# The output's scale and shift in an RWKV-7 recurrence: scale into ScalarE's copy, shift onto the bonus, on one Trainium2 core

## The chip, the cores and the metric

The kernel runs on one core of a Trainium2 chip. The metric is the device time of one execution in microseconds. Of the kernel before, three executions were timed: 2039.26, 2049.12 and 2057.95 us, median 2049.12.

The names in rows and code: PE is TensorE, DVE is VectorE, ACT is ScalarE, POOL is GpSimd, SP is SyncE, which issues the loads.

## The reference, cut to what matters

The program is a chain of an RWKV-7 mixer, a short convolution and a second block. The change concerns the mixer alone. It has 512 positions and 2048 inner channels, in 32 heads of 64.

```python
y = wkv7_scan(rh, heads(decay), kh, vh, kk, kk * ah)
y = head_group_norm(y, lnx_w, lnx_b)       # (y - mean) * rsqrt(var + GN_EPS) * w + b, per head of 64
bonus = (jnp.sum(rh * kh * r_k, axis=-1, keepdims=True) * vh)
y = (y + bonus.reshape(bsz, t, D_INNER)) * jax.nn.silu(g)
out = y @ w_out
```

So each output channel gets a scale w and a shift b after its normalisation, then the bonus is added, then the gate multiplies. The scale and the shift are constants per channel.

## The kernel before, in words

Channels lie on partitions, 128 at a time, which is two heads; positions lie on the free axis. `rwkv_phase` walks over 16 such pairs of heads (`IC` = 16), and a step of its loop works on three pairs at once: it solves the recurrence of pair c by chunks of 64 positions, it prepares the keys, rates, decays and values of pair c+1, and it finishes the outputs of pair c-1. Each engine has its own written-out program of the step, and semaphores tie them together. No scheduler reorders anything: an engine does its operations in the order of the code, and one that waits holds all behind it.

What a step does on each engine, as far as the change and the prediction speak of it:

- TensorE: the scores of pair c (L995, 64 matmuls with `bet`, then 64 with `kd`), five levels of the chunk inverse (L1021 and L1033), in between parts of the dense products for the keys and the values of pair c+1 (L949 to L953). The products for the keys go into the bank `GK`, which `bonus` of pair c was read from, so they wait for `bonus`. In the last step the output projection fills these places instead (L1083 to L1089), and it waits for `y_hi` and `y_lo`, the two halves of the gated outputs.
- VectorE: it begins with `invT` (L1382), read from the scores, then masks and adds of the five levels (L1368, L1373) with copies of the state (L1342) between them. Then come the preparations of pair c+1: `kk` (L1286), `tha` (L1303), `phi` and `rh` (L1439, L1441), `rt` (L1291), `kap` (L1309), `bet` (L1316), `kd` (L1278), and last `bonus` (L1322) and a first state copy. `bonus` has two buffers, used in turn. The one that step c writes for pair c+1 is the one that pair c-1 used, and it is free when the addition of pair c-1 has read it (semaphore `plus`).
- ScalarE: copies from PSUM and the activation functions. `outputs` (L838, L839) copies the outputs of pair c-1 to `yc` and their squares to `yv`; the mean has already gone from the values. Later `output_log` and `output_root` make the inverse deviation in `yv` (semaphore `yrs`). The copies `swapT` (L832) belong to the levels of the inverse.
- GpSimd: a mask (L711), the splits of three tiles in a high and a low half (`halved`, L641 and L644), small products (L666, L672, L677), a split of weights (L689), and at the end of the step the tail of pair c-1, `finished`: `yc` times `yv` (L695), scale and shift (L698), plus the bonus (L702), times the gate (L705). Between two of its operations it waits for the semaphore of the one before.

Pairs 14 and 15 have their tail on VectorE (`finished` there, L1326, L1329, L1332). In the last step GpSimd splits the gated outputs instead (`y_lo`, L660).

`mixpar` holds eight numbers per channel; `chan(c, 6)` is the column of the scales of pair c and `chan(c, 7)` that of its shifts, both already halved for the gate. SyncE's loads are not touched by the change; they wait for `rt`, `bon` and the splits.

Of the kernel before, what the change touches and what calls it, by code (L numbers as in the profile page):

```python
# [6 lines left out]
ALU = mybir.AluOpType  # L7
ACT = mybir.ActivationFunctionType
# [100 lines left out]
def apart(eng):  # L109

    eng.nop(nofuse=True)
# [406 lines left out]
def rwkv_phase(K):  # L518
    nc, ins, bank, psum, C, V = (K[n] for n in ("nc", "ins", "bank", "psum", "C", "V"))
    eps, gate, lerp, hidden, mixpar, sbt = (K[n] for n in ("eps", "gate", "lerp", "hidden", "mixpar", "sbt"))  # L520
    out_raw, out_hi, out_lo = K["ring"]
    y, D = K["y"], K["dense"]
    with ExitStack() as ctx:
        S = Sems(nc, ctx, "mix")
# [4 lines left out]
        def placed(name):  # L529
            at = -(-nc.sbuf_base // 32) * 32  # L530
            return sbt(ctx, name, [P, T]), at
# [5 lines left out]
        rt, bonus = sbt(ctx, "rt", [P, 2, T]), sbt(ctx, "bonus", [P, 2, T])  # L537
# [28 lines left out]
        yc = sbt(ctx, "yc", [P, T])  # L566
        yv, yv_at = placed("yv")
# [6 lines left out]
        chan = lambda n, i: mixpar[:, n, i:i + 1]  # L574
# [15 lines left out]
        parity = lambda ap: ap.rearrange("p (b j t) -> p b j t", j=2, t=HD)  # L590
# [17 lines left out]
        def more(c):  # L608

            return not (isinstance(c, int) and c >= IC - 2)  # L610
# [24 lines left out]
        def _(pool):  # L635
# [11 lines left out]
            def key_halves(n):  # L647
                need(pool, S("kd"), n)
                need(pool, S("bet"), n)
                halved("nsq", n)  # L650
# [35 lines left out]
            def key_weights(n):  # L686
# [2 lines left out]
                pool.tensor_scalar(wts["k"][0][:, :], raw["k"][:, :], 1.0, 0.0, ALU.mult, ALU.add)\  # L689
                    .then_inc(S("whi_k"), 1)  # L690

            def finished(c, p):
                pool.wait_ge(S("yrs"), c + 1)
                apart(pool)
                pool.tensor_tensor(yc[:, :], yc[:, :], yv[:, :], ALU.mult).then_inc(S("yn"), 1)  # L695
                pool.wait_ge(S("yn"), c + 1)
                apart(pool)
                pool.tensor_scalar(yc[:, :], yc[:, :], chan(c, 6), chan(c, 7), ALU.mult, ALU.add).then_inc(S("affine"), 1)  # L698
                pool.wait_ge(S("affine"), c + 1)
                pool.wait_ge(S("bonus"), c + 1)  # L700
                apart(pool)
                pool.tensor_tensor(yc[:, :], yc[:, :], bonus[:, p, :], ALU.add).then_inc(S("plus"), 1)  # L702
                pool.wait_ge(S("plus"), c + 1)
                apart(pool)
                pool.tensor_tensor(gate[:, c, :], gate[:, c, :], yc[:, :], ALU.mult).then_inc(S("gated"), 1)  # L705

            def reads_masked(c):
                pool.wait_ge(S("la"), 2 * c + 2)
                pool.wait_ge(S("inv0"), 2 * c + 2)
                apart(pool)  # L710
                pool.tensor_tensor(LA[:, :, :, 1, :], LA[:, :, :, 1, :], over2(C["score_mask"][:, HD:2 * HD]), ALU.mult)\  # L711
                    .then_inc(S("la_reads"), 1)

            def step(c, p=None):
                q = c % 2 if p is None else p
                last = c == IC - 1
                reads_masked(c)
                if not last:
                    key_halves(c + 1)
                    prepare(c + 1, 1 - q)  # L720
                if last:
                    pool.wait_ge(S("inv0"), 2 * IC)
                    out_halves(range(10))
                if c > 0:
                    halved("ysq", c - 1)
                if not last:
                    rate(c + 1)
                if more(c):
                    key_weights(c + 2)
                if not last:  # L730
                    read_halves(c + 1)
                    chunk_ends(c + 1, 1 - q)
                    if c > 0:
                        finished(c - 1, 1 - q)
# [12 lines left out]
        def _(act):  # L747
# [86 lines left out]
            def outputs(c):  # L834
                act.wait_ge(S("y_mm"), c + 1)
                need(act, S("gated"), c)
                y_banks = psum[:, 2:4, 0:half].rearrange("p j (b t) -> p b j t", t=HD)
                act.activation(parity(yc[:, :]), y_banks, ACT.Copy).then_inc(S("y"), 1)  # L838
                act.activation(parity(yv[:, :]), y_banks, ACT.Square).then_inc(S("ysq"), 1)  # L839

            def out_split(g):
# [9 lines left out]
            def step(c, p=None):  # L851
# [25 lines left out]
                if not first:  # L877
                    outputs(c - 1)
# [377 lines left out]
        def _(dve):  # L1256
# [67 lines left out]
            def finished(c, p):  # L1324
                dve.wait_ge(S("yrs"), c + 1)
                dve.tensor_tensor(yc[:, :], yc[:, :], yv[:, :], ALU.mult).then_inc(S("yn"), 1)  # L1326
                dve.wait_ge(S("yn"), c + 1)
                dve.wait_ge(S("bonus"), c + 1)
                dve.scalar_tensor_tensor(out=yv[:, :], in0=yc[:, :], scalar=chan(c, 6), in1=bonus[:, p, :],  # L1329
                                         op0=ALU.mult, op1=ALU.add).then_inc(S("plus"), 1)  # L1330
                dve.wait_ge(S("plus"), c + 1)
                dve.scalar_tensor_tensor(out=gate[:, c, :], in0=yv[:, :], scalar=chan(c, 7), in1=gate[:, c, :],  # L1332
                                         op0=ALU.add, op1=ALU.mult).then_inc(S("gated"), 1)

            def masked(dst, src, sem):
                dve.tensor_tensor(dst.rearrange("p b k t -> p b (k t)"), pairs(src), over(C["score_mask"], TB),
# [1163 lines left out]
```

## Time and profile before

| | us |
|---|---|
| median of three timed executions | 2049.12 |
| their lowest and highest | 2039.26, 2057.95 |
| the profiled execution | 2050.97 |
| its span, first to last instruction | 2049.2 |
| mean granted TensorE clock | 0.971 |
| recurrence, first `bonus` to last `bonus` start | 270.1 to 807.1 |

The profile shows one execution by engine, with start and duration of each instruction, the idle time before it and what released it. All stretches and starts below are microseconds from the start of the span. A number in square brackets at the end of a row of a timeline is idle time of that engine just before the instruction.

### The profile page before, as it was taken

To read this page: it belongs to the slowest core of one execution; us is meant where nothing else is said; L and a number is where in the kernel's file an instruction comes from. 1 tells how busy PE (TensorE), PEld (TensorE's weight loads), DVE (VectorE), ACT (ScalarE), POOL (GpSimd) and SP (SyncE) were. 2 spreads that over 40 slices of the span, in tenths; PEclk is the share of its full clock that TensorE was granted. 3 is DMA by queue.
4 is the path that set the end of the run, shared out by engine and by line. 5 is a ranking of instruction groups with operands and counts; after the bars stand their busy time and mean duration, and the time that the engine had idled before them with its cause. 6 is when DMAs were issued, how large, how long until landed. Compare 5 with 4: busy or idle time off the path is not lost.

```text
span 2049.2 us, 43917 instructions
## 1 busy us (share of the span) xinstructions
PE 1890.1 (92%) x18912; PEld 1480.9 (72%) x18912; DVE 1234.7 (60%) x1755; ACT 899.7 (44%) x1400; POOL 313.7 (15%) x298
## 2 busy tenths in 40 slices
PE   4999789999999999799999999999887699999997
PEld 3677567767766677588888888887665478888885
DVE  6562177777777777344555555445557577777522
ACT  5342256656565567333222222334445354444321
POOL 3000034535455355300000000000000000000000
PEclk9999899999999999999999999999999799999998
DMA  3224311111111011142322223221110032323331
GB/s 123 78 83 142 109 48 39 44 35 41 46 41 45 30 41 43 49 155 93 101 95 95 100 93 102 89 98 62 52 42 21 21 114 93 103 92 99 91 94 67
DMA packets 51455, 154.15 MB, mean 75 GB/s; under 512 B 8513, under 2 KB 11073, under 8 KB 51265
## 3 DMA queue, kind: packets, MB, share of 16 engines
q1 hardware_dynamic: 51264, 151.35, 22.8%
q8 instruction: 151, 2.47, 0.5%
q14 instruction: 40, 0.32, 0.0%
HBM read 145.04 MB, written 6.29 MB: 74 GB/s over the span
## 4 chain that ended last, share of the span: by engine, by line
PE 51%; DVE 4%; ACT 1%; issue 0%; DVEq 0%; ACTq 0%
PE bank L1670 15%; PE bank L1669 15%; PE bank L1671 15%; PE bank L1757 1%; PE bank L1758 1%; PE bank L1759 1%; DVE room L2381 0%; PE bank L1794 0%; DVE room L2348 0%; PE bank L1777 0%; PE bank L1838 0%; PE bank L1829 0%; PE bank L1740 0%; PE bank L1805 0%; PE bank L1802 0%
## 5 line engine op out<-in xcount | busy, mean ns | idle before, releaser
L1876 ACT ACTIVATE w_hi<-raw 128x1024 fp32r<-128x1024 f32 (+2 forms) x195 | 197.8, 1015 | 504.7 <-PE bank L1671 458.9
L1669 PE MATMUL bank<-h_hi,w_hi 128*128 128x512 f32 x896 | 349.8, 390 | 0.0
L1671 PE MATMUL bank<-h_hi,w_lo 128*128 128x512 f32 x896 | 348.6, 389 | 0.0
L1670 PE MATMUL bank<-h_lo,w_hi 128*128 128x512 f32 x896 | 348.6, 389 | 0.0
L151 DVE TENSOR_TENSOR w_lo<-raw,w_hi 128x1024 fp32r<-128x1024 f32 (+2 forms) x202 | 236.8, 1173 | 154.7 <-ACT w_hi L1876 154.3
L1670 PEld LDWEIGHTS bank<-h_lo,w_hi 128*128 128x128 f32 x896 | 168.2, 188 | 35.6 <-issue 0.7
L1669 PEld LDWEIGHTS bank<-h_hi,w_hi 128*128 128x128 f32 x896 | 168.2, 188 | 35.3 <-issue 0.7
L1671 PEld LDWEIGHTS bank<-h_hi,w_lo 128*128 128x128 f32 x896 | 168.2, 188 | 35.0
L144 PE MATMUL bank<-xg_hi,g_hi 128*128 128x512 f32 x256 | 103.4, 404 | 21.4 <-DVE g_lo L151 11.8
L1651 POOL TENSOR_SCALAR room<-room 128x512 f32<-128x512 f32 x4 | 3.5, 880 | 703.0 <-ACT room L1945 703.0
L832 ACT ACTIVATE swapT<-invT 64x256 f32<-64x256 f32 x192 | 79.8, 416 | 56.8 <-DVE invT L1373 52.9
L145 PE MATMUL bank<-xg_lo,g_hi 128*128 128x512 f32 x256 | 101.9, 398 | 0.0
L146 PE MATMUL bank<-xg_hi,g_lo 128*128 128x512 f32 x256 | 101.6, 397 | 0.0
L151 DVE TENSOR_TENSOR g_lo<-g_raw,g_hi 128x1024 fp32r<-128x1024 f32 x32 | 40.7, 1276 | 88.1 <-ACT g_hi L302 88.0
L1669 PE MATMUL bank<-y_hi,w_hi 128*128 128x512 f32 x224 | 89.2, 398 | 1.3 <-PEq L134 1.3
L1670 PE MATMUL bank<-y_lo,w_hi 128*128 128x512 f32 x224 | 89.8, 401 | 0.0
L1671 PE MATMUL bank<-y_hi,w_lo 128*128 128x512 f32 x224 | 89.1, 398 | 0.0
L1368 DVE TENSOR_TENSOR low<-bank,con 128x512 f32<-128x512 f32 x80 | 55.3, 691 | 53.9 <-PE bank L1021 53.9
L1373 DVE TENSOR_TENSOR invT<-invT,bank 128x512 f32<-128x512 f32 x80 | 55.0, 687 | 52.4 <-PE bank L1033 52.4
L144 PEld LDWEIGHTS bank<-xg_hi,g_hi 128*128 128x128 f32 x256 | 49.6, 194 | 38.6 <-DVE g_lo L151 13.5
L1021 PEld LDWEIGHTS bank<-inv,LA 64*64 64x64 f32 x2560 | 46.0, 135 | 42.5 <-issue 42.5
L302 ACT ACTIVATE g_hi<-g_raw 128x1024 fp32r<-128x1024 f32 x32 | 33.8, 1058 | 90.7 <-PE bank L146 90.5
(390 smaller groups left out, 4363.9 us busy)
## 6 DMA issues: line engine op xcount, KB each, us to landing
raw<-in_w_conv SPq DMA_DIRECT2D x64, 512.0 KB, 3.2
raw<-in_w_up SPq DMA_DIRECT2D x44, 512.0 KB, 3.2
raw<-in_w_out SPq DMA_DIRECT2D x32, 512.0 KB, 3.8
raw<-in_w_in SPq DMA_DIRECT2D x20, 512.0 KB, 3.2
g_raw<-in_w_g SPq DMA_DIRECT2D x16, 512.0 KB, 3.2
g_raw<-in_w_r SPq DMA_DIRECT2D x16, 512.0 KB, 3.7
w_k<-in_w_k SPq DMA_DIRECT2D x16, 512.0 KB, 4.2
w_v<-in_w_v SPq DMA_DIRECT2D x16, 512.0 KB, 3.5
```

What stands on the lines that cost most here:

```text
L144: pe.matmul(out, w_hi[:, w], x_hi[:, k, :], start=(first and n == 0), stop=False)
L145: pe.matmul(out, w_hi[:, w], x_lo[:, k, :], start=False, stop=False)
L146: m = pe.matmul(out, w_lo[:, w], x_hi[:, k, :], start=False, stop=(last and n == len(ks) - 1))
L151: return dve.tensor_tensor(lo, full, hi.bitcast(F32), ALU.subtract)
L832: act.activation(swapT[rows[1 - j], :, :], invT[rows[j], 1, :, :], ACT.Copy).then_inc(S("swap"), 1)
L1021: m = pe.matmul(X[h][rows[j ^ h], cols(b)], LA[rows[j], h, b, 0, :], inv[rows[j], h, b, :], start=True, stop=True)
L1368: dve.tensor_tensor(low[:, :, :, :], heads(0), over2(C["level_mask"][:, lv * HD:(lv + 1) * HD]), ALU.mult).then_inc(S("low"), 1)
L1373: up = dve.tensor_tensor(invT[:, :, :, :], invT[:, :, :, :], heads(half), ALU.add)
L1669: pe.matmul(to, whi, hi, start=begin, stop=False)
L1670: pe.matmul(to, whi, lo, start=False, stop=False)
L1671: last = pe.matmul(to, wlo, hi, start=False, stop=end)
L1876: act.activation(w_hi[:, g % RING, 0:width], raw[:, g % RAW, 0:width], ACT.Copy).then_inc(S("whi"), 1)
```

## The change

The scale is put into ScalarE's copy of the outputs (`yc`), which had none before; `yv`, the squares, is still made from the outputs without it. The shift is added to the finished bonus of the pair by a new operation on GpSimd, `raised`, in the next step behind the mask. The pass that did both in GpSimd's tail goes. The two tails on VectorE lose their scale and shift as well, and become a plain sum and a plain product. The semaphore `affine` goes, `raised` comes in.

```diff
--- before.py
+++ after.py
@@ -689,15 +689,18 @@
                 pool.tensor_scalar(wts["k"][0][:, :], raw["k"][:, :], 1.0, 0.0, ALU.mult, ALU.add)\
                     .then_inc(S("whi_k"), 1)
 
+            def raised(c, p):
+                pool.wait_ge(S("bonus"), c + 1)
+                apart(pool)
+                pool.tensor_scalar(bonus[:, p, :], bonus[:, p, :], chan(c, 7), 0.0, ALU.add, ALU.add)\
+                    .then_inc(S("raised"), 1)
+
             def finished(c, p):
                 pool.wait_ge(S("yrs"), c + 1)
                 apart(pool)
                 pool.tensor_tensor(yc[:, :], yc[:, :], yv[:, :], ALU.mult).then_inc(S("yn"), 1)
                 pool.wait_ge(S("yn"), c + 1)
-                apart(pool)
-                pool.tensor_scalar(yc[:, :], yc[:, :], chan(c, 6), chan(c, 7), ALU.mult, ALU.add).then_inc(S("affine"), 1)
-                pool.wait_ge(S("affine"), c + 1)
-                pool.wait_ge(S("bonus"), c + 1)
+                pool.wait_ge(S("raised"), c + 1)
                 apart(pool)
                 pool.tensor_tensor(yc[:, :], yc[:, :], bonus[:, p, :], ALU.add).then_inc(S("plus"), 1)
                 pool.wait_ge(S("plus"), c + 1)
@@ -715,6 +718,7 @@
                 q = c % 2 if p is None else p
                 last = c == IC - 1
                 reads_masked(c)
+                raised(c, q)
                 if not last:
                     key_halves(c + 1)
                     prepare(c + 1, 1 - q)
@@ -835,7 +839,7 @@
                 act.wait_ge(S("y_mm"), c + 1)
                 need(act, S("gated"), c)
                 y_banks = psum[:, 2:4, 0:half].rearrange("p j (b t) -> p b j t", t=HD)
-                act.activation(parity(yc[:, :]), y_banks, ACT.Copy).then_inc(S("y"), 1)
+                act.activation(parity(yc[:, :]), y_banks, ACT.Copy, scale=chan(c, 6)).then_inc(S("y"), 1)
                 act.activation(parity(yv[:, :]), y_banks, ACT.Square).then_inc(S("ysq"), 1)
 
             def out_split(g):
@@ -1325,12 +1329,10 @@
                 dve.wait_ge(S("yrs"), c + 1)
                 dve.tensor_tensor(yc[:, :], yc[:, :], yv[:, :], ALU.mult).then_inc(S("yn"), 1)
                 dve.wait_ge(S("yn"), c + 1)
-                dve.wait_ge(S("bonus"), c + 1)
-                dve.scalar_tensor_tensor(out=yv[:, :], in0=yc[:, :], scalar=chan(c, 6), in1=bonus[:, p, :],
-                                         op0=ALU.mult, op1=ALU.add).then_inc(S("plus"), 1)
+                dve.wait_ge(S("raised"), c + 1)
+                dve.tensor_tensor(yc[:, :], yc[:, :], bonus[:, p, :], ALU.add).then_inc(S("plus"), 1)
                 dve.wait_ge(S("plus"), c + 1)
-                dve.scalar_tensor_tensor(out=gate[:, c, :], in0=yv[:, :], scalar=chan(c, 7), in1=gate[:, c, :],
-                                         op0=ALU.add, op1=ALU.mult).then_inc(S("gated"), 1)
+                dve.tensor_tensor(gate[:, c, :], gate[:, c, :], yc[:, :], ALU.mult).then_inc(S("gated"), 1)
 
             def masked(dst, src, sem):
                 dve.tensor_tensor(dst.rearrange("p b k t -> p b (k t)"), pairs(src), over(C["score_mask"], TB),
```

On GpSimd the order of a middle step is, before (`yc` is the output, `LA` the masked scores of the next step, `nn_hi` the split of the key norms behind it):

```order
L683 TENSOR_SCALAR ends<-decays 128x8 [waits mix_exp,mix_st]
L695 TENSOR_TENSOR yc<-yc,yv 128x512 [waits mix_yrs]
L698 TENSOR_SCALAR yc<-yc,mixpar 128x512 [waits mix_yn]
L702 TENSOR_TENSOR yc<-yc,bonus 128x512 [waits mix_affine,mix_bonus]
L705 TENSOR_TENSOR gate<-gate,yc 128x512 [waits mix_plus]
L711 TENSOR_TENSOR LA<-LA,con 128x8x64 [waits mix_la,mix_inv0]
L641 TENSOR_SCALAR nn_hi<-nn 128x512 [waits mix_nsq,mix_kd,mix_bet]
```

and now:

```order
L683 TENSOR_SCALAR ends<-decays 128x8 [waits mix_exp,mix_st]
L701 TENSOR_TENSOR yc<-yc,yv 128x512 [waits mix_yrs]
L705 TENSOR_TENSOR yc<-yc,bonus 128x512 [waits mix_yn,mix_raised]
L708 TENSOR_TENSOR gate<-gate,yc 128x512 [waits mix_plus]
L714 TENSOR_TENSOR LA<-LA,con 128x8x64 [waits mix_la,mix_inv0]
L695 TENSOR_SCALAR bonus<-bonus,mixpar 128x512 [waits mix_bonus]
L641 TENSOR_SCALAR nn_hi<-nn 128x512 [waits mix_nsq,mix_kd,mix_bet]
```

The sum with `bonus` follows the product at once, and the pass over `mixpar` stands two places later, on another tile.

On VectorE the tail of pair 14 in the last step was:

```order
L151 TENSOR_TENSOR w_lo<-raw,w_hi 128x1024 [waits dense_whi]
L1326 TENSOR_TENSOR yc<-yc,yv 128x512 [waits mix_yrs]
L1329 SCALAR_TENSOR_TENSOR yv<-yc,mixpar,bonus 128x512 [waits mix_bonus,mix_yn]
L1332 SCALAR_TENSOR_TENSOR gate<-yv,mixpar,gate 128x512 [waits mix_plus]
L1439 TENSOR_TENSOR phi<-bank,con 128x3x64 [waits mix_phi_mm]
```

and is now:

```order
L151 TENSOR_TENSOR w_lo<-raw,w_hi 128x1024 [waits dense_whi]
L1330 TENSOR_TENSOR yc<-yc,yv 128x512 [waits mix_yrs]
L1333 TENSOR_TENSOR yc<-yc,bonus 128x512 [waits mix_raised,mix_yn]
L1335 TENSOR_TENSOR gate<-gate,yc 128x512 [waits mix_plus]
L1441 TENSOR_TENSOR phi<-bank,con 128x3x64 [waits mix_phi_mm]
```

The places are the same, the operations have two operands instead of three.

## Rows read from the trace of the kernel before

**Rows 1.** The page: busy time, share of the span and instructions of each engine.

```profile
PE 1890.1 (92%) x18912; PEld 1480.9 (72%) x18912; DVE 1234.7 (60%) x1755; ACT 899.7 (44%) x1400; POOL 313.7 (15%) x298
```

**Rows 2.** Waits, 230 to 880 us: engine line <- released by: us, times, longest.

```profile
DVE bonus L1322 <- POOL yc L702: 15.2, 12, 1.3
...
PE bank L995 <- issue: 7.5, 6, 2.0
...
PE bank L1089 <- POOL y_lo L660: 3.5, 4, 1.6
```

**Rows 3.** Timeline of GpSimd, step 8: start us, us, instruction [idle before <-releaser].

```profile
581.84 1.29 POOL L695 TENSOR_TENSOR yc<-yc,yv 128x512 f32<-128x512 f32 x1
583.31 2.05 POOL L698 TENSOR_SCALAR yc<-yc,mixpar 128x512 f32<-128x512 f32 x1 [0.18 <-POOL yc L695]
...
602.98 0.62 POOL L641 TENSOR_SCALAR nn_hi<-nn 128x512 fp32r<-128x512 f32 x1 [11.78 <-ACT nn L777]
```

**Rows 4.** Timeline of VectorE over the same tail.

```profile
582.86 0.81 DVE L1291 TENSOR_TENSOR rt<-rraw,decays 128x512 f32<-128x512 f32 x1
583.60 0.68 DVE L1309 TENSOR_TENSOR kap<-kk,decays 128x512 f32<-128x512 f32 x1
584.20 0.68 DVE L1316 TENSOR_TENSOR bet<-tha,cum 128x512 f32<-128x512 f32 x1
584.80 1.09 DVE L1278 TENSOR_TENSOR kd<-kp,cum 128x512 f32<-128x512 f32 x1
587.16 0.69 DVE L1322 TENSOR_TENSOR bonus<-bank,vT 128x512 f32<-128x512 f32 x1 [1.26 <-POOL yc L702]
...
587.96 0.68 DVE L1382 TENSOR_TENSOR invT<-bank,con 128x512 f32<-128x512 f32 x1
```

**Rows 5.** Timeline of TensorE, the scores of the next pair.

```profile
585.42 0.27 PE L995 MATMUL bank<-kap,bet 64*64 64x64 f32 x2
...
586.27 0.33 PE L995 MATMUL bank<-rt,bet 64*64 64x64 f32 x8
```

**Rows 6.** Timeline of all engines, the tail of step 11.

```profile
693.97 1.07 DVE L1291 TENSOR_TENSOR rt<-rraw,decays 128x512 f32<-128x512 f32 x1
...
694.67 1.51 POOL L702 TENSOR_TENSOR yc<-yc,bonus 128x512 f32<-128x512 f32 x1 [0.17 <-POOL yc L698]
...
694.96 1.78 DVE L1309 TENSOR_TENSOR kap<-kk,decays 128x512 f32<-128x512 f32 x1
...
696.33 1.54 POOL L705 TENSOR_TENSOR gate<-gate,yc 128x512 f32<-128x512 f32 x1
...
696.66 1.75 DVE L1316 TENSOR_TENSOR bet<-tha,cum 128x512 f32<-128x512 f32 x1
...
698.57 0.40 PE L995 MATMUL bank<-kap,bet 64*64 64x64 f32 x8 [1.71 <-DVE bet L1316]
...
698.95 0.68 DVE L1322 TENSOR_TENSOR bonus<-bank,vT 128x512 f32<-128x512 f32 x1
```

**Rows 7.** Groups of ScalarE: xcount | busy us, mean ns | idle before.

```profile
L838 ACT ACTIVATE yc<-bank 128x512 f32<-128x512 f32 x13 | 7.9, 605 | 9.5 <-PE bank L1065 9.5
...
L771 ACT ACTIVATE kk<-bank,mixpar 128x512 f32<-128x512 f32 x11 | 7.6, 687 | 18.3 <-PE bank L953 18.3
```

**Rows 8.** Timeline of ScalarE in step 8.

```profile
575.79 0.86 ACT L832 ACTIVATE swapT<-invT 64x256 f32<-64x256 f32 x2 [0.39 <-DVE invT L1373]
```

**Rows 9.** Group of VectorE, its own tails.

```profile
L1329 DVE SCALAR_TENSOR_TENSOR yv<-yc,mixpar,bonus 128x512 f32<-128x512 f32 x2 | 1.5, 751 | 0.1
```

**Rows 10.** Stretches: us, busy (x) of PE, PEld, DVE, ACT, POOL, PEclk, DMA, GB/s.

```profile
697.50:700.00 2.50, 1.44 (x57) 1.47 (x61) 2.31 (x4) 0.00 (x0) 0.37 (x1) 0.75 0.63 205
700.00:702.50 2.50, 2.07 (x78) 1.95 (x71) 1.93 (x3) 1.25 (x3) 0.02 (x1) 0.57 0.02 7
```

**Rows 11.** Timeline of TensorE, the longest pause inside its scores.

```profile
446.26 0.21 PE L995 MATMUL bank<-kap,kd 64*64 64x64 f32 x1 [2.02 <-issue]
```

**Rows 12.** The stretch around and behind that pause, columns as in rows 10.

```profile
445.00:481.00 36.00, 33.71 (x859) 25.84 (x858) 26.88 (x44) 21.91 (x41) 17.27 (x17) 1.00 0.14 41
```

## The prediction

> **What bounds the kernel now.** I read the page first: TensorE is busy for 92% of the span [rows 1], so a change to VectorE, ScalarE or GpSimd counts only where TensorE ends up waiting for it. The page cannot say where that is; the table of waits can. Of the operations that the change touches it names one: VectorE's product `bonus` (L1322) waits for GpSimd's addition L702, 12 times, 15.2 us in all, 1.3 us at the longest [rows 2]. Steps 1 to 14 of the recurrence have this wait in their program (pairs are counted from 0, and step c makes the bonus of pair c+1); in two of them, steps 11 and 14, the buffer was free in time. Then I read one of the twelve on each engine, by the timeline.
>
> GpSimd [rows 3]: its tail runs one operation behind the other, L695 at 581.84, L698 from 583.31 for 2.05 us, then L702, whose end lets `bonus` go. VectorE [rows 4]: `rt`, `kap`, `bet`, `kd` back to back, `kd` done at 584.80+1.09 = 585.89, then nothing until `bonus` at 587.16. That is the wait of 1.27 us. Behind it stands `invT` (L1382) at 587.96, the first operation of the next pair, from which its chain of products and masks starts. TensorE [rows 5]: the scores that `invT` reads begin at 585.42 and the last of them ends at 586.27+0.33 = 586.60, so TensorE is ready for `invT` about 1.3 us before VectorE is. In the twelve steps, then, the wait is on the path, and it is worth at most 587.96-586.70 = 1.26 us a pair (0.1 us for the signal).
>
> The same rows show a second thing. `kd` takes 1.09 us where `kap` and `bet` take 0.68, and L698 takes 2.05 us although it works on the same size. VectorE's products of two SBUF tiles and GpSimd's operations run one after the other here, never at once: `kd` finishes 0.53 us after L698 does (585.36 to 585.89), and `rt` (582.86, 0.81) finishes 0.54 us after L695 (583.13). What has to be asked is therefore not only when L698 goes, but what GpSimd does in its place at 583.31.
>
> **The change part by part.** *L698 goes from GpSimd's tail.* The addition then starts where L698 started, at 583.31: 0.18 us behind L695, as L698 did. At that moment VectorE is in `rt`, and has `kap`, `bet`, `kd` queued. What happens when a GpSimd operation of two tiles starts there is shown by one pair of this trace, whose L698 ran early and free of VectorE [rows 6]. L702 starts at 694.67, in the middle of `rt` (693.97 to 695.04). It is through at 696.18, and `kap`, issued at 694.96, needs 1.78 us and ends at 696.74, 0.56 us behind it. L705 starts at 696.33, in `kap`, ends at 697.87, and `bet`, issued at 696.66, needs 1.75 us and ends at 698.41. So the addition got in between `rt` and `kap`, the last product between `kap` and `bet`, and each held VectorE for 1.1 us. L698 did not do this: it let `kap` and `bet` pass at 0.68 and held `kd` alone for 0.41 us [rows 4]. It has one tile and two per-channel columns to read, the addition has two tiles.
>
> The Trainium skill ("SBUF — State Buffer", section "Who interferes with whom") says that a VectorE operation with two SBUF inputs and a GpSimd operation that reads SBUF exclude each other and that the one that issues first has the shared port to its end. For L702 and L705 the trace agrees (`kap` 1.78, `bet` 1.75 against 0.68). For L698 it does not: it was issued at 583.31, before `kap`, and `kap` was not held. By the page the removal would take a block out from before `kap` as well as put one there.
>
> With the addition at 583.31 all follows from rows 6 by the same distances. `bet` ends 698.41-694.67 = 3.74 us behind it, at 587.05 (before: 584.88). `bonus` starts 698.95-694.67 = 4.28 us behind it, at 587.59 (before: 587.16), with no wait left. TensorE's scores start 0.16 us behind `bet` (698.41 to 698.57), at 587.21, and need 586.60-585.42 = 1.18 us and about 0.08 for the signal; VectorE has done `bonus` and `st` by 588.4 too. `invT` starts at 588.47 instead of 587.96: **0.51 us later**, although the wait of 1.27 us is gone. The stall hasn't been removed, it has moved in front of `kap` and `bet` and has grown. For the 12 pairs: +6.1 us. From both sides: the full wait gained is -1.26 a pair (-15); +0.9 a pair (+11) if the scores come as late after `bet` as rows 6 have it.
>
> *The other two steps.* In step 11, that of rows 6, the addition would come about 0.9 us earlier and gain; in step 14, whose VectorE queue has a split of weights in place of the wait, it would lose some. Bounds -1.5 and +1; I take 0.
>
> *The new `raised` on GpSimd*, one pass over `bonus` behind L711: 15 of the 16 stand in front of `nn_hi`, for which GpSimd sits idle 11.78 us [rows 3], so even 2.05 us (L698's own time) is hidden. What the next operations wait for is on ScalarE. Without this cover it would cost 0.7 to 2 us a pair. In the last pair it stands in front of the splits `y_lo`, and TensorE waits for those, 4 times, 3.5 us [rows 2]: a shift of the row by one pass, 0.8 us, bounds 0 and 2.
>
> *The scale in ScalarE's copy*: a copy with a scale per channel takes 0.687 us, this one takes 0.605 [rows 7]: 0.08 us more, 16 times. In 15 pairs it lies ahead of a `swapT` for which ScalarE sits idle 0.39 us [rows 8], hidden; in the last it is on the chain, +0.1. Without cover 1.3 us.
>
> *VectorE's own two tails* (of pairs 14 and 15, in the last step and behind it): two three-operand operations each become a plain sum and a plain product; 0.751 us [rows 9] to some 0.68 (`kap`'s time [rows 4]) is 4 x 0.07 = -0.3 us. Bounds -0.6 and 0.
>
> *TensorE's clock.* The new pause in front of the scores is at most 587.21-585.42 = 1.8 us, less the matmuls of the step before that still run at 585.42, so some 1.5 us. After the pause of 1.71 us in rows 6 the granted clock fell: 0.75 and 0.57 in the two stretches that follow [rows 10], the lower level, 1.2 GHz, for part of each; 0.25x2.5+0.43x2.5 = 1.7 us of full-speed work is missing. After the pause of 2.02 us at 446.26 it stayed at 1.00 [rows 11, 12]. So a pause of this length can cost up to 1.7 us or nothing. It may also give something back: TensorE's pauses for "issue" in the second half of its scores (6 of them, 7.5 us [rows 2], 2.02 the longest [rows 11]) come right behind the new pause and may pass under it. Bounds for both together: 13x1.7 = +22 and -7.5. I take +2, that is three falls (5) against half of those pauses (3 to 4).
>
> *Sum*: 6.1 + 0 + 0.8 + 0.1 - 0.3 + 2 = +8.7. The profiled execution took 2050.97 us, of which 2049.2 are its span; it lies 1.85 above the median of 2049.12. I forecast 2050.97 + 8.7 - 1.85 = **2057.8 us**, 0.4% more.
>
> **The rivals.**
> *Held as L698 is held.* If the addition lets `kap` and `bet` pass and gets in before `kd`, `kd` waits for 584.80+1.28 = 586.1 and ends at 586.6, `bonus` starts at 586.5, 0.65 us earlier: 12 x 0.65 = -8, so 2041. For it: L698 did just this at this instant in all twelve steps. Against: rows 6.
> *The stall simply goes.* VectorE keeps its pace, the addition is through before `kd` is, and all 1.26 us are gained 12 or 13 times: -16, 2033. For it: 15.2 us of waits. Against: nowhere in this trace do the two engines run such operations side by side.
> *The clock falls in front of every pair* (this ends on the slow side). It is the lower level after each new pause of 1.5 us. From 1.4 us on a pause has been followed by it here, and not always; if it follows 13 times, +6.7+22 = 2078. It decides from some 8 falls on: then the kernel is slower by over 1%. Against: 2.02 us passed without one.
> *Nothing moves*: the splits and stalls absorb either sign, 2049.
>
> **How the numbers follow.** Lock handed over between `rt` and `kap`, few falls of the clock: 0.50. Held as L698: 0.15. Stall gone: 0.12. Clock falls at most pairs: 0.13. Nothing: 0.10. The range from 2039 to 2075 leaves out most of the full gain and the far end of the clock's case, about 2 in 10; it also has to take in that runs of before differ by 19 us. A measurement of this kernel tells a change of about 1% from none: 20 us. The full gain of 16 us doesn't reach that and the clock's case does from eight falls on: faster 0.04, within 1% 0.84, slower 0.12.
>
> **What would show it.** In the profile after: the wait of `bonus` for GpSimd is gone from the table; `kap` and `bet` take some 1.7 us each where they took 0.68; `kd` 0.68; TensorE's scores L995 wait for `bet`, 13 times 1.5 us; the addition starts 0.18 us after the product. If `kap` stays at 0.68 and `kd` grows to 1.8, the first rival holds, and if all three stay at 0.68 the second. If the granted clock of the recurrence is near 0.9 the third. I am wrong if the time is below 2039.

## The result, and the profile after

The changed kernel takes 2058.65 us (median of 20 runs, 2050.23 to 2073.03), the kernel before 2047.76 us (median of 20 runs, 2036.87 to 2057.95). The ratio is 1.0057, with a 95% interval from 1.004 to 1.0073: between 8 and 15 us more, by a change that takes an operation out of the tail that VectorE waits for.

The profiled execution of the changed kernel took 2050.23 us and is the fastest of its twenty; its span of 2048.5 us is not longer than that of before. So the two profiles are compared by stage, not by span. From the first `invT` to the last, the stage that the change touches, it is 537.13 us before (270.75 to 807.88) and 545.19 us after (270.93 to 816.12).

Waits of the changed kernel between 230 and 880 us (engine line <- released by: us, times, longest), to be set beside [rows 2]:

```profile
DVE low L1370 <- PE bank L1025: 58.9, 78, 2.6
...
PE bank L999 <- DVE bet L1320: 23.5, 14, 1.8
...
PE bank L1093 <- POOL y_lo L660: 4.2, 6, 1.4
...
PE bank L999 <- issue: 3.7, 3, 1.7
```

The 15.2 us of `bonus` behind GpSimd are gone, and TensorE has a wait that it had only in the step of [rows 6]: its scores (now L999) wait for `bet`, 14 times, 23.5 us.

The rows of GpSimd, VectorE and TensorE at the end of step 8 of the changed kernel, to be set beside [rows 3, 4, 5] (rows of ScalarE and of TensorE's earlier work left out):

```profile
587.44 1.29 POOL L701 TENSOR_TENSOR yc<-yc,yv 128x512 f32<-128x512 f32 x1
588.46 0.81 DVE L1295 TENSOR_TENSOR rt<-rraw,decays 128x512 f32<-128x512 f32 x1
588.89 1.53 POOL L705 TENSOR_TENSOR yc<-yc,bonus 128x512 f32<-128x512 f32 x1 [0.17 <-POOL yc L701]
589.20 1.77 DVE L1313 TENSOR_TENSOR kap<-kk,decays 128x512 f32<-128x512 f32 x1
590.57 1.53 POOL L708 TENSOR_TENSOR gate<-gate,yc 128x512 f32<-128x512 f32 x1
590.89 1.75 DVE L1320 TENSOR_TENSOR bet<-tha,cum 128x512 f32<-128x512 f32 x1
592.56 0.68 DVE L1282 TENSOR_TENSOR kd<-kp,cum 128x512 f32<-128x512 f32 x1
592.79 0.34 PE L999 MATMUL bank<-kap,bet 64*64 64x64 f32 x8 [1.80 <-DVE bet L1320]
...
593.16 0.68 DVE L1326 TENSOR_TENSOR bonus<-bank,vT 128x512 f32<-128x512 f32 x1
...
594.01 0.69 DVE L1384 TENSOR_TENSOR invT<-bank,con 128x512 f32<-128x512 f32 x1
```

It is the picture of [rows 6], now in all 14 steps that have the tail: the addition goes ahead of `kap`, the product (the gate's) ahead of `bet`, 1.1 us each, and `bonus` starts here 593.16-588.89 = 4.27 us behind the addition.

How the loss is spread over a step is best read from VectorE's own timeline, cut at three operations: `invT` (the step's first), the first masked `low` behind it, and `rt`. These are means over steps 1 to 13 of each profiled execution, and in the last column the length of step 14, in us, worked out from the starts:

```
                         invT to low   low to rt   rt to next invT   step    step 14
before                       3.55        27.29          5.22         36.05    36.17
changed                      3.55        27.32          5.60         36.48    38.72
changed, second profile      3.44        27.25          5.60         36.30    38.37
pass kept (below)            3.28        27.27          5.11         35.66    35.98
```

The profile of before had a disturbed step, the one of [rows 6]. The experiment with the pass kept has the same tail on both engines and no such step, so it stands here for an undisturbed "before". Against it a step of the changed kernel is 0.82 us longer (0.64 in its second profile): 0.50 between `rt` and `invT`, 0.27 (0.16) between `invT` and `low`, and nothing in the long middle. From the first `invT` to the last it is 545.19 and 542.45 us against 531.78, so 13 and 11 us more, of which step 14 alone has 2.7 and 2.4.

The 0.50 is the same in step after step. The 0.27 is not: the profile of before has 3.55 there as well, and in each profile single steps lie 1 us and more above its shortest. What is regular in it is 0.11 us, by the shortest steps: 3.05 before, 3.16 in the changed kernel. TensorE's rows behind the scores of step 9 say why. Before, these are the first of the six key products and the first level of the inverse:

```profile
588.00 0.47 PE L949 MATMUL bank<-lerp_k_hi,w_k_hi 128*128 128x512 f32 x1 [0.44 <-DVE bonus L1322]
...
590.26 0.69 PE L1021 MATMUL bank<-inv,LA 64*64 64x64 f32 x32 [0.64 <-DVE inv L1387]
```

In the changed kernel, the last of the six and the first level:

```profile
596.08 0.40 PE L957 MATMUL bank<-lerp_k_hi,w_k_lo 128*128 128x512 f32 x1
596.41 0.69 PE L1025 MATMUL bank<-inv,LA 64*64 64x64 f32 x32
```

Before, TensorE waited for VectorE twice there, 1.1 us in all. Now it comes to the first level straight from its key products and VectorE waits for it.

In step 14 the loss is larger for a pause of TensorE inside the second half of its scores, which both kernels have. Before:

```profile
772.48 0.28 PE L995 MATMUL bank<-kap,kd 64*64 64x64 f32 x3 [1.35 <-issue]
```

and changed:

```profile
779.77 0.28 PE L999 MATMUL bank<-kap,kd 64*64 64x64 f32 x3 [1.65 <-issue]
```

It ends 0.77 us after the start of `invT` before and 2.37 us after it in the changed kernel, whose scores start later: `low` comes 5.11 us after `invT` in place of 3.50. The other 0.66 us of the step lie between `rt` and the next `invT` (6.66 against 6.00).

### The profile page after: what moved, and what is told of

It reads as the page before. It is cut to its first block, busy times and chain, and to the rows that moved or that the text cites. A ratio compares the mean times of both kernels' runs of the same rounds, so it can differ in the third digit from the quotient of the medians.

```text
span 2048.5 us, 43921 instructions
## 1 busy us (share of the span) xinstructions
PE 1879.9 (92%) x18912; PEld 1471.9 (72%) x18912; DVE 1255.9 (61%) x1755; ACT 901.2 (44%) x1400; POOL 324.9 (16%) x300
## 4 chain that ended last, share of the span: by engine, by line
PE 51%; DVE 4%; ACT 1%; issue 0%; DMA 0%; DVEq 0%; ACTq 0%
PE bank L1672 15%; PE bank L1673 15%; PE bank L1671 15%; PE bank L1759 1%; PE bank L1760 1%; PE bank L1761 1%; DVE room L2383 0%; PE bank L1796 0%; DVE room L2350 0%; PE bank L1779 0%; PE bank L1840 0%; PE bank L1831 0%; PE bank L1742 0%; PE bank L1807 0%; PE bank L1804 0%
```

## The experiments

Theory A is the prediction's: VectorE's products of two SBUF tiles and GpSimd's operations exclude each other, GpSimd takes its turn in the gap between two of VectorE's, and without L698 the addition takes its turn before `kap` and the product before `bet`. Theory B: the loss comes from what was added, the `raised` pass and the scale in ScalarE's copy. Each of the twelve runs was timed beside the kernel before on the same chip, in three groups on three chips; a ratio is always to that kernel before. The microseconds given with a ratio are worked out from it.

**Only the pass taken out, nothing put in.**

```diff
-                pool.tensor_scalar(yc[:, :], yc[:, :], chan(c, 6), chan(c, 7), ALU.mult, ALU.add).then_inc(S("affine"), 1)
-                pool.wait_ge(S("affine"), c + 1)
                 pool.wait_ge(S("bonus"), c + 1)
-                apart(pool)
                 pool.tensor_tensor(yc[:, :], yc[:, :], bonus[:, p, :], ALU.add).then_inc(S("plus"), 1)
```

> The kernel before with only the pass L698 taken out of GpSimd's tail and nothing put in its place: the 14 pairs finished on GpSimd get neither scale nor shift. Theory A (order of the two engines: the addition, now started inside rt, gets in before kap, and the product before bet): as slow as the changed kernel, +8 to +12 us against before; kap 1.78 and bet 1.75 us, kd 0.68, no wait of bonus for GpSimd. Theory B (the loss comes from what was added, the raised pass and the scale in ScalarE's copy): with nothing added the wait of 1.27 us is simply gained, -12 to -16 us, kap and bet 0.68.

Measured: ratio 1.003 (1.0012 to 1.0047), 6.1 us more than before. The wait that it has in every step where the kernel before had it once, by its waits between 230 and 880 us:

```profile
PE bank L992 <- DVE bet L1313: 21.6, 14, 1.6
```

And the end of a step on VectorE, from its timeline (start, busy us, engine, line, operation):

```profile
445.95 1.78 DVE L1306 TENSOR_TENSOR kap<-kk,decays 128x512 f32<-128x512 f32 x1
447.65 1.76 DVE L1313 TENSOR_TENSOR bet<-tha,cum 128x512 f32<-128x512 f32 x1
449.33 0.68 DVE L1275 TENSOR_TENSOR kd<-kp,cum 128x512 f32<-128x512 f32 x1
```

A kernel that does less and adds nothing is slower than before, by the stall that A names. The size was under A's range, so it was run once more, beside the changed kernel:

> The kernel before with the pass L698 alone taken out, once more (14 pairs get neither scale nor shift), beside the changed kernel: the first time it came out 6 us above before, between Theory A's +8 to +12 and nothing. Theory A: within 3 us of the changed kernel. If half of the loss comes from the added work (Theory B in part), 4 us or more below it.

> The changed kernel itself, beside the others on the same chip, so that the differences from it can be read: +8 to +14 us against before by every theory.

Measured: 1.0031 (1.0014 to 1.0048), 6.3 us, for the pass taken out; 1.004 (1.0025 to 1.0055), 8.2 us, for the changed kernel. They overlap (medians 2054.09 and 2054.62 us). Removal alone accounts for at least most of the loss; if the added work costs anything, it is some 2 us, which these runs don't resolve. One place where it shows is the last step, in front of `y_lo`: TensorE's wait for it is 2.4 us in both profiles of the pass taken out and 4.2 us in both of the changed kernel.

**The pass kept, all of the added work kept too.**

```diff
                 pool.wait_ge(S("yn"), c + 1)
+                apart(pool)
+                pool.tensor_scalar(yc[:, :], yc[:, :], chan(c, 6), chan(c, 7), ALU.mult, ALU.add).then_inc(S("affine"), 1)
+                pool.wait_ge(S("affine"), c + 1)
                 pool.wait_ge(S("raised"), c + 1)
```

> The changed kernel, with the pass of scale and shift put back into GpSimd's tail (so the 14 pairs finished there get both twice): ScalarE's scale and the new raised pass stay. Theory A: as before, -1 to +2 us; kap and bet 0.68, kd 1.09, bonus waits 1.27 us for GpSimd again, 12 to 14 times. Theory B: all of the added work is still there, so the loss stays, +8 to +12 us or more.

Measured: 0.9999 (0.9982 to 1.0017). The wait of VectorE is back, by its waits between 230 and 880 us:

```profile
DVE bonus L1329 <- POOL yc L708: 16.4, 13, 1.3
```

ScalarE's scale and the new pass cost nothing that this run can see (by the interval 3.5 us at most). This is the second half of the case against B.

**`raised` with a multiplication in place of the first addition.** The new pass took 2.0 us, longer than L672 of the kernel before, a pass of the same size with two columns and 0.77 us ([rows 3] leaves 11.78 us for it, so the prediction didn't need its time). The values are the same.

```diff
-                pool.tensor_scalar(bonus[:, p, :], bonus[:, p, :], chan(c, 7), 0.0, ALU.add, ALU.add)\
+                pool.tensor_scalar(bonus[:, p, :], bonus[:, p, :], 1.0, chan(c, 7), ALU.mult, ALU.add)\
```

> The changed kernel with raised as times 1 plus the shift in place of plus the shift plus 0; the values are the same. Theory A: the pass falls from 2.0 to some 0.7 us, and as 15 of the 16 stand in front of an idle GpSimd the time stays: +8 to +12 us against before, the same as the changed kernel within 2 us (the last one stands ahead of the splits y_lo, worth up to 1.3). Theory B (the slow raised pass costs): 5 us or more below the changed kernel.

Measured: 1.0046 (1.0028 to 1.0064), 9.5 us, the same as the changed kernel. The instructions on `bonus`, first of the changed kernel and then of this one (ns min/median/max, first and last start):

```profile
L695 POOL TENSOR_SCALAR bonus<-bonus,mixpar x16: 1990/1997/2009, 274.2 to 819.4; 128x512 f32<-128x512 f32 x16
```

```profile
L695 POOL TENSOR_SCALAR bonus<-bonus,mixpar x16: 691/696/710, 274.8 to 823.6; 128x512 f32<-128x512 f32 x16
```

2.0 us against 0.70 us, 16 times, and no gain: the pass is hidden, as predicted, and B is out as the cause of the loss. Only the last of the sixteen can be seen: TensorE's wait for `y_lo` is 3.3 us here.

**Where GpSimd takes its turn.** L698 had let `kap` and `bet` pass. The prediction named its two per-channel columns and its single tile as what sets it apart from the addition. Three kernels ask which it is. The first is the changed kernel with an idle pass without a column in the tail:

```diff
+                pool.tensor_scalar(yc[:, :], yc[:, :], 1.0, 0.0, ALU.mult, ALU.add).then_inc(S("affine"), 1)
+                pool.wait_ge(S("affine"), c + 1)
                 pool.wait_ge(S("raised"), c + 1)
```

> The changed kernel with an idle pass over yc in GpSimd's tail, times 1 plus 0 as constants of the instruction: same place and size as L698, but no per-channel column to read. Theory A1 (GpSimd waits at every gap of VectorE for each thing it reads, so L698 let kap and bet pass because it first read its two columns): without columns the pass gets in between rt and kap, the addition before bet, the product before kd: kap some 1.1 us, bet and kd some 1.75, and the step is the slowest of all, 0.8 us a step, +10 to +14 us against before. Theory A2 (a pass with one tile as input just lets VectorE's sums and products go first, columns or not): kap and bet stay at 0.68, kd 1.09, time as before.

Measured: 1.0054 (1.0034 to 1.0073), 11 us more. The end of a step, timelines of GpSimd and then of VectorE:

```profile
444.89 0.87 POOL L704 TENSOR_SCALAR yc<-yc 128x512 f32<-128x512 f32 x1 [0.16 <-POOL yc L701]
...
445.94 1.50 POOL L708 TENSOR_TENSOR yc<-yc,bonus 128x512 f32<-128x512 f32 x1 [0.17 <-POOL yc L704]
...
447.58 1.54 POOL L711 TENSOR_TENSOR gate<-gate,yc 128x512 f32<-128x512 f32 x1
```

```profile
445.20 1.09 DVE L1316 TENSOR_TENSOR kap<-kk,decays 128x512 f32<-128x512 f32 x1
446.22 1.76 DVE L1323 TENSOR_TENSOR bet<-tha,cum 128x512 f32<-128x512 f32 x1
447.91 1.76 DVE L1285 TENSOR_TENSOR kd<-kp,cum 128x512 f32<-128x512 f32 x1
```

Three turns, three products held, as A1 has it, in 12 of the 14 steps (in the other two GpSimd's tail ran earlier and the pass met none of the three). A pass with one column was tried twice, first with the shift (the part in GpSimd's tail; the scale is in ScalarE's copy):

```diff
-                pool.tensor_scalar(yc[:, :], yc[:, :], chan(c, 6), chan(c, 7), ALU.mult, ALU.add).then_inc(S("affine"), 1)
+                pool.tensor_scalar(yc[:, :], yc[:, :], chan(c, 7), 0.0, ALU.add, ALU.add).then_inc(S("affine"), 1)
```

> The kernel before with the scale in ScalarE's copy as in the change, and the pass in GpSimd's tail left with the shift alone, one per-channel column and a constant. Theory A1: one gap of VectorE for the column (between rt and kap), the next for the tile: bet is held (some 1.1 us), then kd by the addition (some 1.75), kap 0.68; bonus 0.3 us earlier than before: -4 to +1 us. Theory A2: as before, kap and bet 0.68, kd 1.09, 0.

Measured: 1.002 (1.0003 to 1.0037), 4 us more. `kap` 0.68 and `bet` 1.09 were as A1 expects, but `kd` was 0.68 and the pass took 2.75 us: it was the slow form of two additions and was still running when `kd` was over, so it was `bonus` that waited, 1.75 us. The expectation failed on the form of the operation, not on the first turn. So again with a multiplication, from the changed kernel (the part in GpSimd's tail; ScalarE's copy is plain again, `raised` has its multiplication first, and VectorE's own tails take the scale):

```diff
+                pool.tensor_scalar(yc[:, :], yc[:, :], chan(c, 6), 0.0, ALU.mult, ALU.add).then_inc(S("affine"), 1)
+                pool.wait_ge(S("affine"), c + 1)
                 pool.wait_ge(S("raised"), c + 1)
```

> As the one-column run before, but with a multiplication first in both passes of GpSimd, since a pass of two additions took 2.0 us or more and hid what was asked: scale as a pass (times its column, plus 0) in the tail, ScalarE's copy plain, shift by raised as times 1 plus its column. Theory A1 (one gap of VectorE for each column, the next for the tile): kap 0.68, bet 1.09, kd 1.75, the pass 1.4 us, bonus 0.3 us earlier than before: -4 to +1 us. Theory A2 (a column costs no turn): kap 1.09, bet and kd 1.76 as without a column, +8 to +12 us.

Measured: 0.9992 (0.9975 to 1.0009), level with before and inside A1's range. The same step, GpSimd and then VectorE:

```profile
441.49 1.45 POOL L704 TENSOR_SCALAR yc<-yc,mixpar 128x512 f32<-128x512 f32 x1 [0.18 <-POOL yc L701]
```

```profile
441.78 0.68 DVE L1316 TENSOR_TENSOR kap<-kk,decays 128x512 f32<-128x512 f32 x1
442.38 1.09 DVE L1323 TENSOR_TENSOR bet<-tha,cum 128x512 f32<-128x512 f32 x1
443.40 1.77 DVE L1285 TENSOR_TENSOR kd<-kp,cum 128x512 f32<-128x512 f32 x1
```

No column: `kap` is held first. One: `bet`, in 13 of 14 steps. Two, in the kernel before [rows 4] and with the pass kept: `kd`, in 13 and 14 of 14. Each column that the pass reads lets one more product of VectorE's queue go by. That the column itself is what is read in the gap is the simplest account of it; no row shows the read.

**The addition two places later.**

```diff
                 pool.wait_ge(S("raised"), c + 1)
+                pool.wait_ge(S("kap"), c + 3)
```

> The changed kernel, and GpSimd's addition also waits for VectorE's kap of the next pair, so that it starts inside bet and not inside rt. Theory A: kap and bet 0.68, the addition gets in between bet and kd, kd some 1.8 us, bonus 0.65 us earlier in a step than before: -6 to -9 us against before, 16 to 20 below the changed kernel. Theory B: a later addition can only cost, +10 us or more. Theory C (the pause in front of the scores and the clock are what costs): the pause is gone as well, so as A in time, but then kap and bet would not matter; told apart by the granted clock, which A expects unchanged near 0.98 of the span.

Measured: 0.9997 (0.9983 to 1.001). This was to be 6 to 9 us below before and is level with it. The turns are as expected, by VectorE's timeline of that step:

```profile
440.05 0.68 DVE L1314 TENSOR_TENSOR kap<-kk,decays 128x512 f32<-128x512 f32 x1
440.65 0.68 DVE L1321 TENSOR_TENSOR bet<-tha,cum 128x512 f32<-128x512 f32 x1
441.25 1.77 DVE L1283 TENSOR_TENSOR kd<-kp,cum 128x512 f32<-128x512 f32 x1
442.94 0.68 DVE L1327 TENSOR_TENSOR bonus<-bank,vT 128x512 f32<-128x512 f32 x1
...
443.73 0.67 DVE L1385 TENSOR_TENSOR invT<-bank,con 128x512 f32<-128x512 f32 x1
...
447.22 0.69 DVE L1371 TENSOR_TENSOR low<-bank,con 128x512 f32<-128x512 f32 x1 [0.76 <-PE bank L1026]
```

One added wait, which puts the addition behind `bet` in place of before `kap`, takes the changed kernel's whole loss away, which bears out A's account of the loss. Theory C shares the pause with A, and the pause is gone here too; its other part, the clock, is not what costs: the mean granted clock over the executions is 0.9745 for the changed kernel in the second comparison and 0.9743 for the kernel before beside it (0.9746 and 0.9741 for this run). But the last row shows why there is no gain: `low` comes 3.49 us after `invT`, where an undisturbed step of the kernel before has 3.05.

**The tail out of the way altogether.** GpSimd's tail of pair c-1 moves behind the mask of the next step. As two buffers for the bonus would no longer do, VectorE makes it in the tile of the rates, dead by then, and `raised` moves it into its buffer.

```diff
-                pool.tensor_scalar(bonus[:, p, :], bonus[:, p, :], chan(c, 7), 0.0, ALU.add, ALU.add)\
+                pool.tensor_scalar(bonus[:, p, :], tha[:, :], chan(c, 7), 0.0, ALU.add, ALU.add)\
...
                 reads_masked(c)
+                if 1 < c < IC - 1:
+                    finished(c - 2, q)
                 raised(c, q)
...
-                    if c > 0:
+                    if c == IC - 2:
                         finished(c - 1, 1 - q)
...
-                need(act, S("bet"), n)
+                need(act, S("raised"), n)
...
-                need(dve, S("plus"), n - 1)
-                dve.tensor_tensor(bonus[:, p, :], GK[:, :], vT[:, :], ALU.mult).then_inc(S("bonus"), 1)
+                dve.wait_ge(S("bet"), n + 1)
+                dve.tensor_tensor(tha[:, :], GK[:, :], vT[:, :], ALU.mult).then_inc(S("bonus"), 1)
```

> The changed kernel with GpSimd's tail of pair c-1 moved behind the mask of the next step (the place of raised), where it meets VectorE's reads of PSUM; the bonus is made in the tile of the rates and raised moves it to its buffer. Only pair 13 keeps its place. Theory A: rt, kap, bet, kd all 0.68, no wait of bonus: 1.26 us a step against before, -12 to -16 us, some 25 below the changed kernel. Theory D (TensorE's own work or another chain bounds the step, so VectorE's gain is swallowed): -4 to 0 against before, with TensorE's or ScalarE's waits grown less than VectorE's fell.

Measured: 0.998 (0.9962 to 0.9998), 4 us below before. Theory A's 12 to 16 us did not come, D's did. A step of it on VectorE's timeline, and then TensorE's pause in the same step:

```profile
409.52 0.68 DVE L1322 TENSOR_TENSOR bet<-tha,cum 128x512 f32<-128x512 f32 x1
410.12 0.68 DVE L1284 TENSOR_TENSOR kd<-kp,cum 128x512 f32<-128x512 f32 x1
410.72 0.68 DVE L1328 TENSOR_TENSOR tha<-bank,vT 128x512 f32<-128x512 f32 x1
...
412.10 0.69 DVE L1386 TENSOR_TENSOR invT<-bank,con 128x512 f32<-128x512 f32 x1 [0.50 <-PE bank L1001]
...
416.71 0.69 DVE L1372 TENSOR_TENSOR low<-bank,con 128x512 f32<-128x512 f32 x1 [1.88 <-PE bank L1027]
```

```profile
416.23 0.39 PE L1027 MATMUL bank<-inv,LA 64*64 64x64 f32 x11 [1.17 <-issue]
```

Between `rt` and `invT` VectorE's chain is free and 1.47 us shorter, and then it stands before TensorE: first for the scores (0.50), then for the first level (1.88, of which 1.17 is a pause of TensorE for nothing that the profile shows). Which part of the tail mattered was asked with the pass of scale and shift left in the late tail and `raised` as a plain move (the two main places, against the late tail):

```diff
+                pool.tensor_scalar(yc[:, :], yc[:, :], chan(c, 6), chan(c, 7), ALU.mult, ALU.add).then_inc(S("affine"), 1)
...
-                act.activation(parity(yc[:, :]), y_banks, ACT.Copy, scale=chan(c, 6)).then_inc(S("y"), 1)
+                act.activation(parity(yc[:, :]), y_banks, ACT.Copy).then_inc(S("y"), 1)
```

> The late tail of the run before (behind the mask of the next step), but with the pass of scale and shift kept in it, the plain copy in ScalarE, and raised as a plain move. It asks what the change is worth where the tail meets none of rt, kap, bet, kd. Theory A: nothing, -2 to -6 us against before as with the late tail alone. If scale and shift on their new places are worth something by themselves, it is 2 us or more slower than the late tail.

Measured: 0.9984 (0.9969 to 1.0), the same. Where the tail meets nobody, the change is worth nothing that can be seen. Last, TensorE's first place gets three of the key products in place of six, and the next three places one more each:

```diff
-                fill(keys, 6, 10)
+                fill(keys, 3, 10)
...
-                fill(keys, 4, 3)
+                fill(keys, 5, 3)
```

> The late tail with three of the six key products that TensorE does between the scores and the first level of the inverse moved behind the next three places, one each. Theory E (with VectorE's wait gone, the first level is late because TensorE is still at these six, 0.23 us each, and at pauses in its own supply of instructions): the first masked low comes 0.4 to 0.7 us earlier after invT, -6 to -14 us against before. Theory F (TensorE is busy the whole step and any place is as good): the same as the late tail, -2 to -6, the time reappearing at the three later places.

Measured: 1.0006 (0.9987 to 1.0025), 1 us above before and slower than either theory expected (its interval just reaches F's). `low` came 0.45 us earlier, and the time was back, and more, at the three places that took a product each. The same table as above, for the runs that this turns on:

```
                         invT to low   low to rt   rt to next invT   step    step 14
pass kept                    3.28        27.27          5.11         35.66    35.98
addition after kap           3.92        27.23          4.44         35.59    37.16
late tail                    4.17        27.19          3.64         35.00    38.20
late tail, with the pass     4.25        27.20          3.78         35.23    37.35
late tail, three products    3.72        28.03          3.78         35.54    38.05
```

What leaves the third column comes back in the first: 0.67 us against 0.64 with the addition after `kap`, 1.47 against 0.89 with the late tail. Step 14 takes back another 1.2 to 2.2 us. Each line is one profiled execution, and the first column differs by 0.27 us between before and pass kept, which have the same tail, so a difference of that size in it shows nothing.

## Why the prediction was right, and where its steps were off

- *The number.* 2057.8 us was forecast, 2058.65 measured; +8.7 against a measured +11 (8 to 15), and +8.2 in the second comparison. The case that was given 0.50 is the one that happened. That the time itself is met within 1 us is in part luck: the forecast started from 2049.12 us, the median of three executions, and twenty have 2047.76, and two terms that were wrong, below, cancel: +2 for the clock, and nothing for what the late scores do behind `invT`.
- *The addition gets in before `kap`, the product before `bet`.* Right in all 14 steps, and to 0.01 us in the distances taken from [rows 6]: `kap` 1.77, `bet` 1.75, `bonus` 4.27 us behind the addition (4.28 forecast). The removal alone and the delayed addition show that this is the cause. The rival "held as L698 is held" did not happen. Of the two differences that the prediction named between L698 and the addition, the columns and the single tile, the runs with no and one column leave the columns: with none, a pass over one tile gets in before `kap` as the addition does.
- *`invT` 0.51 us later a step.* Measured 0.50 from `rt` against the pass kept, 0.39 against the profiled before with its disturbed step.
- *Nothing behind `invT`.* Here a term was missing. As the scores start later and TensorE's six key products follow them, TensorE comes to the first level 0.11 us later than VectorE's chain did (3.16 us at the shortest where it was 3.05), 1.4 us over steps 2 to 14. And a pause of its own that the wait of `bonus` had in part covered now shows: 1.5 us more in step 14. Between the two profiles compared above the mean grew by 0.27 us a step; what of that is more than the 0.11 is not settled, since the profiled before has the same mean as the changed kernel.
- *The other two steps at 0.* They were sized from one disturbed execution. In the changed kernel step 11 is like the others; step 14 is 0.66 us longer between `rt` and `invT`, within the bound of 1, and with the pause in front of that 2.2 to 2.7 us longer in all.
- *The clock, +2 for falls of it and pauses that pass under the new one.* The pauses came in front of the scores, 14 times, 1.7 us in the mean. The granted clock fell after one of them in the recurrence. The window of that fall (us, busy of PE, PEld, DVE, ACT, POOL, PEclk, DMA, GB/s) has a mean granted clock of 0.57, near the lower of its two levels:

```profile
518.50:522.50 4.00, 3.83 (x129) 3.74 (x130) 3.42 (x7) 1.31 (x3) 0.09 (x1) 0.57 0.26 99
```

  That is one fall where three were taken. In the second profile of the changed kernel it is one again and with the faster `raised` four; the kernel before has three in this stretch, one of them that of [rows 10], and the pass kept none. So the falls scatter between executions, the rival in which it falls at most pairs is out, and no cost of the clock shows: its means over the executions are those given above, 0.9745 and 0.9743. The pauses for "issue" inside the scores went from 7.5 to 3.7 us, half, as was taken, though not the one in step 14.
- *`raised` hidden.* Right, though it took 2.0 us and not the 0.8 that L672 would suggest: with 1.3 us less for each of the 16 the time did not fall.
- *ScalarE's scale.* 0.08 us forecast; the copy's group now has a mean of 0.696 us against 0.605 [rows 7], hidden (ScalarE's groups between 400 and 1350 us):

```profile
L842 ACT ACTIVATE yc<-bank,mixpar 128x512 f32<-128x512 f32 x13 | 9.1, 696 | 9.6 <-PE bank L1069 9.6
```

- *VectorE's own two tails.* The sum and the product take 0.691 and 0.694 us; some 0.68 was forecast, in place of 0.751 [rows 9].
- *The last pair's pass, 0.8 us.* TensorE's wait for `y_lo` is 4.2 us in the table of waits above where it was 3.5 [rows 2], so 0.7 us more by that view. It was 2.4 us with the pass only taken out, so a single pair of profiles gives this to 1 us at best.
- *The sum once more.* An estimate from the figures above: 13 steps of 0.50 between `rt` and `invT` and 0.66 in step 14, 7.2; 13 first levels of 0.11, 1.4; the pause in step 14, 1.5; `y_lo`, 0.7; VectorE's tails, -0.3. That is 10.5 us, inside the measured 8 to 15.
- *The prices of the two fast rivals.* "The stall simply goes" was priced at 16 us and "held as L698" at 8, by the sentence that the wait is on the path and worth up to 1.26 us a step. Run as experiments these brought 4 us and nothing. The wait was on the path, but TensorE was only 1.1 us ahead at the first level, by the two waits in its rows of step 9, and it used these to cover pauses of its own. The bound should have been read at the first operation that needs TensorE after `invT`, not at `invT`.

What stays open: what TensorE's pauses for "issue" wait for, whether the added work costs the 2 us by which the ratios of the changed kernel and of the bare removal differ, and how much of the swallowed gain is pauses, since each table line rests on one profile.

## What to carry to other kernels

When two engines exclude each other on some operations, an operation in one's queue also decides in which gap of the other the next ones fall: before taking it out, write down what the neighbour is doing at the instant at which the successor will now start, and look in the trace for one place where the two have already met in that way. A wait is worth no more than the distance to whatever is next to be late, and that is read at the next operation which needs the third engine. Work whose result nobody needs for a step belongs where the neighbour reads PSUM or is idle: the late tail is the one version here that comes out below the kernel before beyond its interval, and only just (0.9962 to 0.9998).

## What the runs showed of the hardware that was not expected

- A GpSimd pass over 128x512 took 1997 ns as two additions (plus its column, plus 0) and 696 ns as a multiplication and an addition (times 1, plus its column), with the same values. The column's place is not what matters: a multiplication by the column, plus 0, took 693 ns where VectorE did not hold it.
- A GpSimd pass with two per-channel columns started first and still let two products of VectorE go by; with one column it let one by, and with none it let none by. The Trainium skill ("SBUF — State Buffer", section "Who interferes with whom") gives the shared port to the one that issues first, for its whole instruction. For operations on two tiles and for the pass without a column the traces agree (`kap` 1.78 and 1.09 us); for the passes with a column they do not.
- VectorE's products run one behind the other with 0.60 us from start to start, and yet GpSimd got in between `rt` and `kap`, `kap` and `bet`, and `bet` and `kd`, each in one of these kernels. A GpSimd sum or product of two tiles then holds the next for 1.1 us, a pass for 0.41 us.
